# A separate step list for each of two mixing layers in a single-core fp32 transformer kernel

## The reference, cut to what matters

```python
def token_mixing(x, shift, scale, ...):
    h = rmsnorm(x, g_pre) * (1.0 + scale) + shift
    proj = h @ w_in                      # 1024 x 8352, split below
    ...
    ya = rmsnorm(differential_attention(...), g_subln) @ da_w_o      # 4 heads, two score maps each
    q, kv from rmsnorm(mla_cq) @ w_uq and rmsnorm(mla_ckv) @ w_ukv, with rope
    yb = softmax_attention(q, k, v_b) @ mla_w_o                      # 8 heads
    yc = (sc_b * causal_dwconv(sc_c * sc_u, sc_conv)) @ sc_w_o       # 3 taps
    u = causal_dwconv(cf_a * sigmoid(cf_g), cf_conv) + cf_conv_b     # 31 taps, width 512
    yd = silu(layernorm(u)) @ cf_w_o
    merged = g0 * ya + g1 * yb + g2 * yc + g3 * yd                   # g = sigmoid(gates)
    return rmsnorm(merged @ w_mix_out, g_post)

for l in range(2):
    x = x + gate1 * token_mixing(x, ...)
    x = x + gate2 * channel_mixing(x, ...)
```

## Time and profile before

| | us |
|---|---|
| median of 3 runs | 3313.85 |
| lowest and highest | 3311.53, 3317.24 |
| the profiled execution's own time | 3317.55 |
| its span, first to last instruction | 3315.8 |
| busy: PE, PEld, DVE, ACT | 3170.8, 3082.9, 2488.2, 1779.0 |
| mixing of layer 0, on TensorE | 37.2 to 387 |
| mixing of layer 1, on TensorE | 583 to 944 |

### The profile page before, as it was taken

One profiled execution on the slowest core, in us unless ns is written; L12 is line 12 of the kernel. 1 busy time (PEld: TensorE's weight loads), 2 busy tenths in 40 slices (PEclk: granted clock), 3 DMA queues, 4 the chain that ended last, 5 costly groups with the idle time before them and its releaser, 6 DMA issues.

```text
span 3315.8 us, 64468 instructions
## 1 busy us (share of the span) xinstructions
PE 3170.8 (96%) x27118; PEld 3082.9 (93%) x27118; DVE 2488.2 (75%) x3822; ACT 1779.0 (54%) x2723; POOL 3.0 (0%) x6
## 2 busy tenths in 40 slices
PE   6899999989999999989999999999999999998999
PEld 6889999888999999879999989999979999987999
DVE  8888799987887766787676667667667667678766
ACT  4556554555564545665454546455456455456544
POOL 0000000000000000000000000000000000000000
PEclk8999999999999999999999999999999999999999
DMA  7456478444746555435555544555544555543453
GB/s 288 130 178 225 167 277 321 145 126 138 244 173 230 169 189 187 157 99 188 190 184 187 189 134 169 187 182 191 188 137 149 187 184 189 188 165 103 162 190 129
DMA packets 164353, 597.94 MB, mean 180 GB/s; under 512 B 18240, under 2 KB 18272, under 8 KB 163936
## 3 DMA queue, kind: packets, MB, share of 16 engines
q1 hardware_dynamic: 164064, 593.81, 53.3%
HBM read 592.69 MB, written 1.05 MB: 179 GB/s over the span
## 4 chain that ended last, share of the span: by engine, by line
PE 74%; DVE 16%; ACT 6%; issue 2%; DMA 1%; SPq 0%; DVEq 0%; ACTq 0%
PE ps L512 24%; PE ps L513 24%; PE ps L514 24%; DVE wlo L472 4%; ACT whi L460 2%; DVE fa L1769 1%; DVE land L658 1%; DVE fa L2663 0%; DMA land<-w_ada 0%; DMA land<-w_in 0%; DVE tmps L691 0%; DVE h L2017 0%; DVE tmps L689 0%; PE ps L2515 0%; DVE tmps L2372 0%
## 5 line engine op out<-in xcount | busy, mean ns | idle before, releaser
L512 PE MATMUL ps<-h,whi 128*128 128x256 f32 x5280 | 1489.9, 282 | 34.9 <-DVE h L931 13.9
L514 PE MATMUL ps<-h,wlo 128*128 128x256 f32 x5328 | 1491.6, 280 | 0.0
L513 PE MATMUL ps<-h,whi 128*128 128x256 f32 x5280 | 1478.5, 280 | 0.0
L472 DVE TENSOR_TENSOR wlo<-land,whi 128x1024 fp32r<-128x1024 f32 (+1 forms) x1026 | 1210.4, 1217 | 252.1 <-ACT whi L460 250.7
L460 ACT ACTIVATE whi<-land 128x1024 fp32r<-128x1024 f32 (+1 forms) x1026 | 1023.8, 1045 | 155.5 <-PE ps L514 129.2
L512 PEld LDWEIGHTS ps<-h,whi 128*128 128x128 f32 x5280 | 997.1, 189 | 44.0 <-issue 27.2
L514 PEld LDWEIGHTS ps<-h,wlo 128*128 128x128 f32 x5328 | 1005.7, 189 | 0.0
L513 PEld LDWEIGHTS ps<-h,whi 128*128 128x128 f32 x5280 | 997.3, 189 | 0.8
L513 PE MATMUL ps<-y,whi 128*128 128x256 f32 x1472 | 410.9, 279 | 0.0
L512 PE MATMUL ps<-y,whi 128*128 128x256 f32 x1472 | 410.9, 279 | 0.0
L514 PE MATMUL ps<-y,wlo 128*128 128x256 f32 x1472 | 410.9, 279 | 0.0
(11 more groups left out here) (470 smaller groups left out, 2904.1 us busy)
## 6 DMA issues: line engine op xcount, KB each, us to landing
land<-w_gu SPq DMA_DIRECT2D x352, 512.0 KB, 3.6
land<-w_dn SPq DMA_DIRECT2D x176, 512.0 KB, 3.5
land<-w_in SPq DMA_DIRECT2D x136, 512.0 KB, 3.5
land<-w_ada SPq DMA_DIRECT2D x96, 512.0 KB, 4.4
land<-w_up SPq DMA_DIRECT2D x88, 512.0 KB, 3.8
land<-hg_in SPq DMA_DIRECT2D x64, 512.0 KB, 3.5
land<-w_down SPq DMA_DIRECT2D x44, 512.0 KB, 4.1
land<-ple_gate SPq DMA_DIRECT2D x32, 512.0 KB, 3.5
```

Of the source, the lines that this page charges most:

```text
L472: dve.tensor_tensor(w.lo, g.slot(n), w.hi.bitcast(F32), ALU.subtract).then_inc(*D_("w_lo", n))
L512: pe.matmul(out, w.hi, x.hi, start=first, stop=False, skip_group_check=skip)
L513: pe.matmul(out, w.hi, x.lo, start=False, stop=False, skip_group_check=skip)
L514: return pe.matmul(out, w.lo, x.hi, start=False, stop=last, skip_group_check=skip)
```

## The change

The list is laid out anew, and a second one, `MIX1_ORDER`, is written for layer 1. Each holds the same steps as the old one; only their order differs. `layer_steps(lay)` gives the programs, the banks and the order of the weight tiles the list of the layer at hand.

```diff
 MIX_ORDER = """
-    norm:0 cf:0 cf:1 tables:0 conv:0 cf:2 conv:1 lam:0 conv:2 cf:3 scu:0 conv:3 conv:4 qk:0 qk:1 scu:1 conv:5 conv:6
...
+    norm:0 cf:0 cf:1 lam:0 conv:0 cf:2 conv:1 tables:0 conv:2 cf:3 qk:0 conv:3 tables:1 conv:4 scu:0 mla:0 conv:5
...
-def mix_steps():
+MIX1_ORDER = """
+    norm:0 cf:0 cf:1 conv:0 cf:2 conv:1 tables:0 conv:2 cf:3 qk:0 conv:3 conv:4 scu:0 conv:5 tables:1 scu:1 conv:6
...
+def tiled_steps(order):
 
     steps, tiles = [], 0
-    for step in MIX_ORDER.split():
+    for step in order.split():
...
-MIX = mix_steps()
+def mix_steps():
+    return tiled_steps(MIX_ORDER)
+
+def mix1_steps():
+    return tiled_steps(MIX1_ORDER)
+
+MIX, MIX1 = mix_steps(), mix1_steps()
+
+def layer_steps(lay):
+    return MIX1 if lay else MIX
...
-    return [(step, i, 3 if lay and (step, i) == ("cf", LEAD) else bank) for step, i, bank in MIX]
+    return [(step, i, 3 if lay and (step, i) == ("cf", LEAD) else bank) for step, i, bank in layer_steps(lay)]
...
-    lead = [s for s in MIX if s[0] in PROJECTIONS][:LEAD if lay else 1]
+    lead = [s for s in layer_steps(lay) if s[0] in PROJECTIONS][:LEAD if lay else 1]
...
-        for step, i, bank in MIX:
+        for step, i, bank in layer_steps(lay):
```

More of the change, by code:

```diff
@@ L1200 @@
 MIX_ORDER = """
-    norm:0 cf:0 cf:1 tables:0 conv:0 cf:2 conv:1 lam:0 conv:2 cf:3 scu:0 conv:3 conv:4 qk:0 qk:1 scu:1 conv:5 conv:6
-    conv:7 conv:8 qk:2 conv:9 v:0 mla:0 v:1 conv:10 conv:11 mla:1 tables:1 conv:12 mc:0 qk:3 conv:13 mla_square:0
-    da_scores:0 conv:14 da_combine:0 mla_norm:0 conv:15 da_scores:1 conv:16 da_combine:1 da_turn:0 da_scores:2
-    da_values:0 mla_apply:0 da_combine:2 conv:17 scu:2 da_turn:1 da_scores:3 da_combine:3 da_turn:2 mla_square:1 scu:3
-    da_turn:3 da_values:1 uq:0 da_values:2 mla_norm:1 sc_conv:0 sc_conv:1 scb:0 sc_conv:2 sc_conv:3 gate2:0 scb:1
@@ L1206 @@
-    mla_apply:1 conv:18 gate2:1 wo2:0 ya_square:0 da_values:3 wo2:1 ya_square:1 ya_norm:0 merge2:0 merge2:1 gate2:2
-    gate2:3 wo2:2 ya_apply:0 merge2:2 wo2:3 uq:1 merge2:3 uq:2 ya_norm:1 rope:0 ya_apply:1 rope:1 rope:2 uq:3 rope:3
-    rope:4 kr_all:0 ukv:0 conv:19 ukv:1 ukv:2 mv:0 cf_sum:0 ukv:3 mv:1 mla_scores:0 mla_scale:0 gate1:0 mla_scores:1
-    mla_scale:1 mla_scores:2 mla_scale:2 cf_mean:0 mla_turn:0 gate1:1 mla_scores:3 cf_square:0 mla_turn:1 mla_values:0
-    gate1:2 mla_values:1 cf_norm:0 mla_turn:2 mla_scale:3 cf_apply:0 gate0:0 mla_scores:4 mla_scores:5 mla_turn:3
@@ L1216 @@
-"""
-def mix_steps():
+    norm:0 cf:0 cf:1 lam:0 conv:0 cf:2 conv:1 tables:0 conv:2 cf:3 qk:0 conv:3 tables:1 conv:4 scu:0 mla:0 conv:5
+    scu:1 v:0 conv:6 conv:7 conv:8 qk:1 qk:2 conv:9 conv:10 conv:11 conv:12 mla:1 mc:0 conv:13 conv:14 v:1
+    mla_square:0 qk:3 da_scores:0 conv:15 da_combine:0 mla_norm:0 da_scores:1 conv:16 da_combine:1 scu:2 da_turn:0
+    da_scores:2 conv:17 da_combine:2 da_values:0 da_turn:1 da_scores:3 mla_apply:0 da_combine:3 da_turn:2 scu:3
+    mla_square:1 da_turn:3 sc_conv:0 da_values:1 sc_conv:1 ya_square:0 uq:0 scb:0 sc_conv:2 mla_norm:1 sc_conv:3
@@ new lines @@
+    conv:18 da_values:2 scb:1 gate2:0 gate2:1 da_values:3 wo2:0 wo2:1 mla_apply:1 merge2:0 ya_square:1 merge2:1
+    gate2:2 ya_norm:0 gate2:3 wo2:2 wo2:3 ya_apply:0 merge2:2 merge2:3 uq:1 uq:2 ya_norm:1 rope:0 rope:1 ya_apply:1
+    rope:2 uq:3 rope:3 rope:4 kr_all:0 ukv:0 ukv:1 ukv:2 ukv:3 conv:19 mv:0 mla_scores:0 mla_scale:0 mv:1 mla_scores:1
+    cf_sum:0 gate1:0 gate0:0 mla_scale:1 mla_scores:2 mla_scale:2 mla_turn:0 cf_mean:0 cf_square:0 mla_scores:3
+    gate1:1 mla_turn:1 gate1:2 mla_values:0 mla_values:1 mla_turn:2 mla_scale:3 cf_norm:0 mla_scores:4 mla_scores:5
@@ L1221, in mix_steps @@
+"""
+def tiled_steps(order):
     steps, tiles = [], 0
-    for step in MIX_ORDER.split():
+    for step in order.split():
         name, at = step.split(":")
```

24 lines of the change are left out of this document (19 added, 5 removed).

## The result

The changed kernel takes 3294.99 us (median of 4 runs, 3294.72 to 3295.43), the kernel before, run beside it, 3314.55 (4 runs, 3311.53 to 3317.24). The ratio is 0.9939, with a 95% interval of 0.9927 to 0.9952: 19.6 us faster, where I forecast 7.5. That is outside my range of 3297 to 3317. One of the five executions of a kernel further down, e9, took 17554.71 us at a mean granted clock of 0.162, and its ratio goes by the other four.

A forecast was written before the change was run, and what follows sets the result against it. TensorE, busy 3170.8 of 3315.8 us, was taken as the bound, so only its standing or half-clock time could move. The terms summed to -7.5 us, taking the median from 3313.85 to 3306.4 (chance 0.50); range 3297 to 3317.

The forecast's parts named there:

- second attention: Layer 0's second attention: +1 us, bounds 0 and +3, as `gate0:0` no longer covers the wait for `mla_turn:3`.
- Beginning of layer 0: Layer 0's start: 0 us, bounds -1 and +3; TensorE is full, split weights at worst 0.7 us late.
- First attention of layer 0: Layer 0's first attention: -1 us, bounds -5 and +2; `scu:2` fills TensorE's wait but starts at the low clock.
- Ropes of layer 0: Layer 0's ropes: -3.5 us, bounds -6 and 0; VectorE's chain to `kr_all` ends the stretch and starts earlier.
- Ends: Ends of both mixings: -0.5 us layer 0, -0.7 layer 1, with `merge1:0` ahead of the last splits; bounds -2 and +1 each.
- Beginning of layer 1: Layer 1's start: -0.3 us, bounds -4.4 and +3; the hole stays, only `lam` leaves VectorE's queue ahead of the splits.
- First attention of layer 1: Layer 1's first attention: -2.5 us, bounds -6 and +2; `scu:2` and `gate2:0` lie where TensorE waited and ran slow.
- Ropes of layer 1: Layer 1's ropes: 0 us, bounds -2 and +2, since they keep their old order.
- One of my signs of being wrong: Either mixing's end (387 and 944 us) coming forward by less than 1 us or more than 8.
- the closing holes: Rival, first attentions: waits of 7.2 us and half clock go in both layers, -5 and -6; 3299 us, chance 0.18.
- The moved wait: Rival: VectorE still ends both attentions; first attentions give nothing, ropes 1.5; -2 us, 3312, chance 0.22.
- Starved weights: Rival: VectorE splits weights late behind four convolution steps in layer 0; two such places, +8 us, 3322, chance 0.10.

The follow-up runs named there:

- e9: Changed kernel with `gate0:0` moved from the second attention to behind `rope:2` in both layers; 3295.91 us, ratio 0.9938.
- e4: Changed kernel with layer 1's new list used in both layers; 3298.88 us, ratio 0.9948.
- e5: Kernel before with `scu:2` alone moved from behind `da_values:0` to behind `da_combine:1`, both layers; 3317.63 us, ratio 1.0004.
- e18: Kernel before with the new order only from `da_scores:0` to `scb:1`, both layers, convolution count before `da_scores:0` kept; 3313.30 us, ratio 0.9990.
- e6: Kernel before with the old order up to `gate1:0` and each layer's new order from there; 3306.62 us, ratio 0.9971.
- e15: Changed kernel with layer 0's `gate0:0` alone moved to behind `cf_apply:0`; 3298.88 us, ratio 0.9946.

## Why the prediction was wrong

The term that failed most is that of the second attention. I had +1 for layer 0, and for layer 1 no term at all and no reason for that; measured are -3.8 and -3.7. The two make 8.5 us, where the mixings as a whole beat my sum by 10.6. By term:

- *Beginning of layer 0*: 0 forecast, +0.5. Within the bounds. With list 1 (e4) it is +2.9.
- *First attention of layer 0*: -1 forecast, -3.1. The clock did fall by 131 us, but "some 6 us at half speed" was 3.4 here. The step that cost more is that VectorE's chain "then goes on as before less the splits and multiply of `scu:2`": head 3's combine came 3.7 us sooner, because of VectorE's own order too (e5 against e18). The bound of -5 held.
- *Ropes of layer 0*: -3.5 forecast, -0.7. The step "it still has 13 us of work against a chain of 17" was right, and `kr_all` came on time; but I counted the earlier start as a gain of this stretch. It is the first attention's gain, handed on. The two terms together were -4.5 and came to -3.8.
- *Second attention*: "`gate0:0` no longer covers `mla_turn:3`" was true and cost 0.5, or 1.2 with the old head (e6). But I priced the stretch by this one step and never read its other waits: 1.5 us of `gate0:2` and 0.3 of `wo1:3` for banks that merges free, and 0.8 at `cf_norm`, stood to be won in layer 0, and 3.0 us for such banks in layer 1. They are gone in the changed kernel, where others of 0.5 and 0.9 stand, and e6 shows that the new tail alone brings most of the gain. Which step of it does, and what makes up the rest beyond these waits, stays open. e15 shows that the moved `gate0:0` still works as cover, 4.1 us' worth.
- *Ends*: -0.5 and -0.7 forecast, -0.9 and -0.8. Right.
- *Beginning of layer 1*: -0.3 forecast, -1.6. "The hole stays" is right, 4.7 us. Over the kernels with that list it is -1.3 to -1.6 where the low clock behind the hole lasts 3.4 us, as in after, and -0.3 to -0.6 where it lasts 6.8, as before. So the order gives what I had, and the rest is the clock.
- *First attention of layer 1*: -2.5 forecast, -3.9 with 13.7 us of low clock and -6.6 to -7.1 with 6.8. Even -3.9 is more than I counted on VectorE.
- *Ropes of layer 1*: 0 forecast, -0.2. Right.

One of my signs of being wrong came true: the mixing of layer 0 ends at 378.3 and not at 387, 8.6 us sooner, more than the 8 I allowed.

The rule from the Trainium skill that I set against the trace ("TensorE: Matmul & The Clock Gate", section "What's actually happening") would have given -5 for layer 0's first attention; -3.1 lies between it and my -1. The trace agrees with it in part: with the hole filled the low clock ended after 3.4 us and not 13.7, but it fell again, at 130.5 us, though TensorE had been busy for 4.14 of the 6 us ahead of that. I took the row with 0.50 for a fixed property of the whole stretch; the row of after has 0.89 there.

Of the rivals, the closing holes gave 3299 and was nearest, but by luck for the most part: its waits did not go, 7.2 us became 4.5, the first attentions gave 7.0 and not 11, and the second attentions, which it left out as I did, gave 7.5. The moved wait is what happened at the ropes. Starved weights did not show in the changed kernel.
